# Two model blocks in one kernel: the start column of narrow activation tiles, and a place of their own for layer 1's branch halves

## The reference, cut to what matters

```python
hx = modulate(rmsnorm(x, norm_w[l]), shift_x, scale_x)
px = split_proj(hx @ w_in[l])          # 1024 x 11008: ret_*, sc_*, cf_*, att_*, merge gates
pc = split_proj(hc @ w_in[l])          # layer 0; in layer 1 only ret_k, ret_v, att_k, att_v
r, s, f, a = retention, short conv, conformer conv, windowed attention  # each times silu(z), 512 wide
merged = sum(sigmoid(g) * (br @ w_branch[i]) for i, (g, br) in enumerate(zip(gates, (r, s, f, a))))
x = x + gate_x * (merged @ w_out)
```

## Time and profile before

| | us |
|---|---|
| median of 3 runs | 1748.65 |
| the profiled execution | 1751.2 |
| its span (first to last instruction) | 1749.4 |
| TensorE matmuls busy | 1705.1 (97%) |
| TensorE weight loads busy | 1489.2 (85%) |
| VectorE busy | 1394.1 (80%) |
| ScalarE busy | 882.7 (50%) |
| mean granted TensorE clock | 0.995 |

### The profile page before, as it was taken

The page is one execution under the profiler, slowest core; times in us unless marked ns, Lnnn a source line. Parts: engine busy times, 40 slices in busy tenths (PEclk is TensorE's granted clock), DMA queues, the critical chain, the costliest instruction groups (busy, mean ns, idle before and its releaser), DMA issues.

```text
span 1749.4 us, 28134 instructions
## 1 busy us (share of the span) xinstructions
PE 1705.1 (97%) x10612; PEld 1489.2 (85%) x10612; DVE 1394.1 (80%) x2532; ACT 882.7 (50%) x1530; POOL 0.2 (0%) x4
## 2 busy tenths in 40 slices
PE   7999999999999999999999999999999999999998
PEld 4788887777888888897988899998899888889997
DVE  7699996546789998888877699977888668778874
ACT  5322324456233233353446754667765657576563
POOL 0000000000000000000000000000000000000000
PEclk9999999999999999999999999999999999999999
DMA  9683311211767876744333389844555545346553
GB/s 341 209 302 107 96 54 44 97 37 37 253 228 242 280 248 216 241 145 144 121 97 97 97 284 313 268 136 153 189 192 181 182 146 169 117 139 204 184 189 110
DMA packets 224774, 301.32 MB, mean 172 GB/s; under 512 B 6000, under 2 KB 188656, under 8 KB 224256
## 3 DMA queue, kind: packets, MB, share of 16 engines
q1 hardware_dynamic: 224640, 299.52, 51.4%
HBM read 298.45 MB, written 1.05 MB: 171 GB/s over the span
## 4 chain that ended last, share of the span: by engine, by line
PE 47%; DVE 4%; ACT 3%; issue 2%; DMA 0%; DVEq 0%; ACTq 0%
PE bank L699 10%; PE bank L704 10%; PE bank L701 10%; PE bank L1085 3%; PE bank L1087 3%; PE bank L1086 3%; ACT w_hi L1401 1%; PE bank L675 1%; DVE w_lo L2182 1%; PE bank L677 1%; PE bank L676 1%; PE bank L1152 1%; PE bank L1215 1%; PE bank L930 0%; PE bank L1065 0%
## 5 line engine op out<-in xcount | busy, mean ns | idle before, releaser
L2182 DVE TENSOR_TENSOR w_lo<-ring,w_hi 128x1024 fp32r<-128x1024 f32 (+1 forms) x432 | 490.1, 1141 | 180.9 <-ACT w_hi L1401 178.6
L1401 ACT ACTIVATE w_hi<-ring 128x1024 fp32r<-128x1024 f32 (+1 forms) x432 | 425.2, 990 | 176.1 <-PE bank L704 93.3
L699 PE MATMUL bank<-h_hi,w_hi 128*128 128x256 f32 (+2 forms) x2086 | 377.3, 322 | 1.8 <-ACT w_hi L1401 1.5
L704 PE MATMUL bank<-h_hi,w_lo 128*128 128x256 f32 (+2 forms) x2086 | 370.4, 319 | 0.1
L701 PE MATMUL bank<-h_lo,w_hi 128*128 128x256 f32 (+2 forms) x2086 | 370.4, 319 | 0.0
L699 PEld LDWEIGHTS bank<-h_hi,w_hi 128*128 128x128 f32 x2086 | 308.6, 188 | 36.6 <-ACT w_hi L1401 3.7
L704 PEld LDWEIGHTS bank<-h_hi,w_lo 128*128 128x128 f32 x2086 | 309.5, 188 | 29.7 <-DVE w_lo L2182 0.3
L701 PEld LDWEIGHTS bank<-h_lo,w_hi 128*128 128x128 f32 x2086 | 309.5, 188 | 29.6
L1388 ACT ACTIVATE work<-bank 128x512 f32<-128x512 f32 (+1 forms) x134 | 67.2, 520 | 252.0 <-PE bank L704 167.9
L1388 ACT ACTIVATE arena<-bank 128x256 f32<-128x256 f32 (+4 forms) x119 | 55.1, 468 | 202.5 <-PE bank L704 121.9
L2483 DVE SCALAR_TENSOR_TENSOR arena<-arena,params 128x512 f32<-128x512 f32 (+1 forms) x240 | 130.4, 611 | 0.0
(11 more groups left out here) (320 smaller groups left out, 2131.7 us busy)
## 6 DMA issues: line engine op xcount, KB each, us to landing
ring<-in_w_in SPq DMA_DIRECT2D x86, 1024.0 KB, 5.5
arena<-in_ada_w_t SPq DMA_DIRECT2D x96, 512.0 KB, 5.8
ring<-in_ffn_w_up SPq DMA_DIRECT2D x44, 1024.0 KB, 5.1
ring<-in_ffn_w_down SPq DMA_DIRECT2D x20, 1024.0 KB, 5.1
ring<-in_w_branch SPq DMA_DIRECT2D x32, 512.0 KB, 4.7
arena<-in_w_mod_t SPq DMA_DIRECT2D x32, 512.0 KB, 4.6
ring<-in_gla_w_in SPq DMA_DIRECT2D x12, 1024.0 KB, 5.2
ring<-in_w_out SPq DMA_DIRECT2D x8, 1024.0 KB, 6.1
```

Source lines behind the costliest of these rows:

```text
L699: pe.matmul(out[:, 0:n], w[0][:, k, :], hi(k, n), start=k == 0, stop=False)
L704: m = pe.matmul(out[:, 0:n], w[1][:, k, :], hi(k, n), start=False, stop=k == tiles - 1)
L1401: nc.scalar.activation(hi, src, ACT.Copy)\
L2182: step(nc.vector.tensor_tensor(lo, src, hi.bitcast(F32), ALU.subtract), f"lo {u}", *(["used " + stream[w_units[u][0]][0]] if w_units[u][3] ...
```

## The change

`OFF` becomes 32. The rows of `g_hi` become S + 64 = 320 columns long. A function `branch_part(l, lo, b, t)` gives the halves of a branch: for layer 0 the places of before; for layer 1 tiles of 256 columns, high and low side by side, from column 16704 + OFF = 16736, one place for all four branches. ScalarE's and VectorE's splitting and TensorE's branch products use it.

```diff
-OFF = 16
+OFF = 32
...
-        g_hi, g_lo = (tiles_of(h, S + 2 * OFF)[:, :, 0:LATE_N] for h in h_flat)
+        g_hi, g_lo = (tiles_of(h, S + 64)[:, :, 0:LATE_N] for h in h_flat)
...
+        def branch_part(l, lo, b, t):
+
+            if l:
+                at = 16704 + OFF + 2 * S * t + S * lo
+                return arena_r[:, at:at + S]
+            return (branch_lo[b] if lo else branch_hi)[:, t, :]
...
-            def part(h, s0):
-                return lambda k, n: h[:, k, s0:s0 + n]
...
-                            project(f"br {l}.{b}.{2 * i + j}", nx, part(branch_hi, 0), part(branch_lo[b], 0),
+                            project(f"br {l}.{b}.{2 * i + j}", nx, lambda k, n: branch_part(l, 0, b, k), lambda k, n: branch_part(l, 1, b, k),
                                     None if i or j else both_parts(f"br {l}.{b}"), BT)
...
-                        nc.scalar.activation(branch_hi[:, t, 0:nx], branch[b][:, t, 0:nx], ACT.Copy)\
+                        nc.scalar.activation(branch_part(l, 0, b, t), branch[b][:, t, 0:nx], ACT.Copy)\
...
-                        low_part(f"br {l}.{b}.{t}", branch_lo[b][:, t, 0:nx], branch[b][:, t, 0:nx],
-                                 branch_hi[:, t, 0:nx])
+                        low_part(f"br {l}.{b}.{t}", branch_part(l, 1, b, t), branch[b][:, t, 0:nx],
+                                 branch_part(l, 0, b, t))
```

## The result

| | before | after |
|---|---|---|
| median of 6 runs, us | 1748.09 | 1755.96 |
| lowest and highest | 1745.89, 1752.19 | 1754.1, 1757.49 |
| the profiled execution | 1751.2 | 1755.67 |
| its span | 1749.4 | 1753.9 |

The ratio is 1.0041, 95% interval 1.0028 to 1.0055. The forecast was 1730.7 us with a range of 1726 to 1738. The result lies outside it, at the very end of the wide range (1725 to 1756), and on the side of the rival "slower". The medians are 7.9 us apart (interval 4.9 to 9.6), the two profiled spans 4.5 us; the two traces can account for these 4.5 only. The kernel after has four more lines ahead of `project`, so its lines 703, 705 and 708 answer to 699, 701 and 704 before.

What follows compares the result with a forecast made beforehand. TensorE's ns per matmul was taken to bound the kernel. Six savings summed to 21.4 us, less 2.4 and 1.0 gave 18; from the median 1748.65 this made 1730.7 us, range 1726 to 1738 (8 in 10: 1725 to 1756).

Steps and rivals of the forecast that it cites:

- rival "slower": Narrow tiles at 128 bytes conflict more: 120 to 122 ns in FFN, gates and output; 1760 us at 120; chance 0.21.
- the bounds: Unknown narrow pace at 128 bytes: between 113.3 ns, saving 22.9 us, and 120 ns, losing 11 us.
- Term 1: FFN up projections of both layers: 2112 matmuls at 117.8 ns save 4.44 ns each, 9.4 us.
- Term 2: Layer 1's 256-column projections and gates: 1344 of 1632 matmuls save 4.44 ns each, 6.0 us.
- Term 3: Branch products of layer 1: 384 matmuls at 120 ns save 6.67 ns each, 2.6 us.
- Term 4: Output projection of layer 1: 192 matmuls save 4.44 ns each, 0.9 us.
- Term 5: RG-LRU block's gate and input: 384 matmuls go from 120 to 114.2 ns, saving 2.2 us.
- Term 6: GLA's q and k: 192 matmuls, most already at the undisturbed pace; 0.3 us saved.
- Wide groups: Layer 1's 512-wide units, 0.6 us gained or lost, and GLA's v and r rows, -0.9 to +0.9; taken as 0.
- The deductions: Taken off the savings: 2.4 us for split-weight waits in layer 1's merge, 1 us for restarts that settle badly.
- Half effect: Rival: 128 bytes also has two spacings, the slow one after part of the restarts; 1740 us; chance 0.13.
- No effect: Rival: pace follows the restart, not the distance, so the savings vanish; 1748 us, within 2; chance 0.14.

Runs made afterwards that it cites:

- All192: Kernel after the change with OFF = 48 instead of 32, narrow tiles 192 bytes from the weights; 1737.88 us, ratio 0.9935 to the kernel before.
- all0: Kernel after the change with OFF = 0 instead of 32, narrow tiles at distance 0; 1757.88 us, ratio 1.0043 to the kernel before.
- all64: Kernel after the change with OFF = 16 instead of 32, narrow tiles 64 bytes from the weights; 1748.97 us, ratio 0.9988 to the kernel before.
- map1: Separate program of matmul chains after pauses, moving and weight columns varied; 256 wide: 120.00, 117.77, 118.67, 113.33 ns at differences of 0, 16, 32, 48 columns.
- narrow192: All192 with the 258-column tiles of the RG-LRU input starting at column 4; 1738.07 us, ratio 0.994 to the kernel before.
- map2: Matmul chains alone, after 16 pause lengths or forerunners of other widths; after pauses 117.77 ns at column 16 and 113.33 at 48.
- map3: Matmul chains alone: 30 to 32 matmuls, a forerunner, 32 more without a pause; column 16 chains ran at 117.8 or 113.3 ns.

## Why the prediction was wrong, step by step

- **What bounds the kernel, and which term moves: right.** TensorE's spacing sets the time. FFN up follows the map one to one, and no engine, queue or wait took over.
- **No new wait: right** for layer 1's low halves (1.66 us ahead of the first branch products, 1.6 before).
- **The step that failed** is the choice between the bounds: "I choose the lower end because the excess falls from 6.7 (0) to 4.4 or 0 (64) ... 128 is as far as one can be modulo 256." It takes the excess as falling with distance and as symmetric. Measured, over 113.33 ns: 6.7 at 0, 4.4 or 0 at 64, **5.3 (in places 6.7) at 128**, 0 or 4.4 at 192. Two of the four points were in the trace, one of them with two values; a line through them had nothing to stand on, and the two points that it spanned were not the ends of anything.
- **The terms, at the pace measured.** Term 1, 2112 matmuls: forecast 9.4 us saved, measured 1.8 lost (0.88 + 0.91). Term 2: forecast 6.0 saved. The 1056 narrow matmuls of projections and mixers (those four gate units with them) went from a mean of 116.5 to 118.65, 2.1 us more, and the wide ones cost 0.9; the two stages grew by 1.7 only, since part of it went into time in which TensorE waits there anyway (below). The 288 matmuls that had locked at 113.4 went to 118.7 too: I costed them at nothing, and at a bad pace of 128 they lose 288 x 5.3 = 1.5 us. Term 3, the branches: forecast 2.6 saved, measured 384 x 1.2 = 0.5 saved, given back by the gates. Term 4: 0.9 saved against 0.15 lost. Term 5: 2.2 saved against 0.4 lost. Term 6: 0.3 saved against 0.3 lost, GLA's q and k having stood at 113.4.
- **Waits in layer 1.** One that shrank, from the waits of TensorE between 762 and 1008 us (waited for: us in total, times, longest), before and then after:

```profile
PE bank L988 <- DVE arena L2676: 1.1, 1, 1.1
```
```profile
PE bank L992 <- DVE arena L2680: 0.6, 1, 0.6
```

It gives back 0.5. Over the whole kernel TensorE is 6.1 us longer busy and the span 4.5 us longer, so 1.6 us of the dearer matmuls lay beside work that TensorE waited for before.
- **Wide groups: "if the cost goes on growing by the same step it loses 0.6".** That side was right: 229.1 to 232.8, 240 x 3.7 = 0.9 us. The rows of GLA moved by nothing (231.1, 230.7).
- **The deductions** for the merge (2.4) and bad restarts (1.0) had nothing to be taken from here. All192, where the pace did fall, shows that the first was right in size and named the wrong wait. From the first branch product to the RG-LRU block's first gate its matmuls are 4.4 us cheaper than before, but longer gaps give 2.1 of them back. The wait for split weights stayed at 1.7 us; what grew most is the wait for the merged sum ahead of the output projection, 0.93 us in the earlier trace rows:

```profile
1117.39 0.36 PE L679 MATMUL bank<-arena_r,w_hi 128*128 128x256 f32 x1 [1.84 <-ACT arena_r L1746]
...
1115.30:1117.39 2.09, 0.25 (x4) 0.08 (x2) 2.06 (x5) 0.44 (x2) 0.00 (x0) 1.00 0.99 341
```

VectorE is busy for 2.06 of these 2.09 us (second row): a faster TensorE does run into it there.
- **The rival "slower" came true**, with the turning point that it names: "turns at a pace of about 117.7 and is 5 us slower at 119". Measured were 118.7 and 4.5 us of span. What had spoken for it, wide tiles and rows growing dearer from 0 to 64, was read rightly. *Half effect*: no run shows a pace of 113.3 at 128 for weights of 128 columns; the two patterns there are 118.7 and 120. *No effect*: half of it is true, history does pick the pace at 64, but not the whole; all0, all64, after and all192 differ in a constant alone and run FFN at 120, 117.8, 118.7 and 113.3.
- **For FFN the size of the prize was right, and the place wrong.** At 192 bytes FFN's two stages are 8.9 us shorter than before (9.4 forecast). In the profiled spans all192 is 13.7 us below the kernel before (1735.7 against 1749.4), but 1.2 of these lie in layer 0, which no change touched; 12.5 are left of a sum of 21.4. The rest is missing in the wide tiles of layer 1 (233 for 229: 240 x 4 = 1.0 us), in the 258-column tiles (120.9), in parts of layer 1 and its branches that still lock at 117.8, and in the 2.1 us of waits above.
- The Trainium skill (TensorE: Matmul & The Clock Gate, Part 2, step 1) gives TensorE two independent read ports and says that loading weights takes no read bandwidth from the running matmul. The measurements differ: map1's chains hold nothing but matmuls and their weight loads, and moving either operand changes the spacing from 113.3 to 120. The measurement decides that the two reads are not without effect on each other's time; by what path they meet no run here shows.

**Open.** Why 28 and 48 columns and no neighbour are undisturbed is not settled; the runs give the map, not the circuit. Nor is it settled what picks the pattern behind a pause. How often an execution locks well or badly was not counted. All192 and narrow192 run the same code up to the end of the merge, whose stage takes 112.56 us in one and 111.95 in the other (the four gate units ahead of it run at 117.8 and 113.6), and single executions of the kernel before differ by 6 us; that a share of the 7.9 us between the medians, beyond the 4.5 seen, is such locking is argued, not shown.

## What to carry to other kernels

When back-to-back matmuls with a new weight load each bind a kernel, measure their spacing as the difference of starts in the timeline, per shape and per offset, before moving anything: a program of a hundred short chains maps it in one run, and each point is worth several chains after different matmuls, since one distance can hold two spacings. Never interpolate between two such points, and ask of each existing fast stretch what the change does to it. Tiles of different widths want different offsets (256 columns: 48 columns from the weights; 512: none), so give each width its own start. Where the matmuls do get cheaper, look at the waits behind them: part of the gain can end there.

## What the runs showed of the hardware, unexpected

- The spacing of fp32r matmuls with a weight load of 128 columns each depends on the distance of moving tile and weights modulo 256 bytes: for 256 columns 120.0, 117.8, 118.7 and 113.3 ns at 0, 64, 128 and 192 bytes, for 512 columns 226.7, 228.8, 233.3 and 233.4. Absolute columns make no difference in 16 pairs.
- The good places for 256 columns are single ones, as far as tried (steps of 4, and single steps around these two): 28 and 48 give 113.33, the columns beside them 119 to 123 (map2).
- At one distance two patterns hold themselves (113.3 and 117.8 ns at 64 and at 192 bytes, 118.7 and 120 at 128). A pause gave the slow one at 16 columns in all 16 chains of map2 and in 23 of 33 of map3, and the fast one at 48 in 16 of 16 and 13 of 15; without a pause one to three matmuls of another width can flip it, and how many came before matters.
- Weights of only 16 columns have their own map: 116.7, 113.3, 113.3, 117.8 ns at 0, 64, 128 and 192 bytes.
